# Prompt attention with closing banks freed by ScalarE, later combinations and evenly spread maximum units

## The reference

```python
def masked_softmax(s, mask):
    s = jnp.where(mask, s, NEG)
    m = jnp.max(s, axis=-1, keepdims=True)
    e = jnp.where(mask, jnp.exp(s - m), 0.0)
    return e / jnp.maximum(jnp.sum(e, axis=-1, keepdims=True), 1e-30)
...
    g = jax.nn.sigmoid(gates.astype(jnp.float32)).reshape(b, tq, NSA_GROUPS, HPG, 3)
    o = g[..., 0:1] * o_cmp + g[..., 1:2] * o_slc + g[..., 2:3] * o_win
```

## Time and profile before

| | us |
|---|---|
| median of 3 runs | 2638.7 (2637.68 to 2643.01) |
| profiled execution, device time | 2634.91 |
| profiled execution, span of instructions | 2633.1 |
| TensorE busy over the span | 2270.2 |
| stage of the prompt's attention | 446 to 803 |

### The profile page before, as it was taken

How to read it: one execution, slowest core, us unless ns; L and a number is a source line. 1 busy time by engine, 2 the same in 40 slices (tenths; PEclk the granted TensorE clock), 3 DMA queues, 4 the chain that set the end, 5 groups by cost and what they waited for, 6 DMA issues and landing times. The chain is left out here.

```text
span 2633.1 us, 32958 instructions
## 1 busy us (share of the span) xinstructions
PE 2270.2 (86%) x13162; PEld 1924.0 (73%) x13162; DVE 1049.5 (40%) x1988; ACT 556.9 (21%) x986; POOL 450.1 (17%) x174
## 2 busy tenths in 40 slices
PE   5598896888886878887779999797999999999997
PEld 3477684333335757887668888796998989898996
DVE  1754074454532222455511111415443444344345
ACT  2476163333331101111111110103111101101110
POOL 0211010133441001110011100212222212211120
PEclk9798897888896578988889999898999999999998
DMA  7111253000003222110123322212211111111101
GB/s 277 45 44 55 52 189 118 1 1 0 1 0 136 93 89 71 50 41 27 42 76 101 103 68 84 99 30 53 65 49 33 49 49 43 39 49 49 33 33 66
DMA packets 135814, 164.57 MB, mean 63 GB/s; under 512 B 11058, under 2 KB 108083, under 8 KB 131108
## 3 DMA queue, kind: packets, MB, share of 16 engines
q1 hardware_dynamic: 125366, 109.85, 13.8%
q0 software_dynamic: 7552, 48.16, 5.5%
q10 hardware_dynamic: 2768, 4.70, 0.5%
HBM read 149.10 MB, written 17.87 MB: 63 GB/s over the span
## 5 line engine op out<-in xcount | busy, mean ns | idle before, releaser
L242 PE MATMUL psall<-hT,ring_short 128*128 128x344 f32 x1536 | 506.3, 330 | 64.0 <-POOL ring_short L237 41.4
L244 PE MATMUL psall<-hT,ring_short 128*128 128x344 f32 x1536 | 499.2, 325 | 0.0
L243 PE MATMUL psall<-work_short,ring_short 128*128 128x344 f32 x1296 | 420.1, 324 | 14.4 <-issue 14.4
L237 POOL TENSOR_TENSOR ring_short<-ring,ring_short 128x2048 fp32r<-128x2048 f32 (+3 forms) x49 | 197.7, 4035 | 1028.9 <-DVE ring_short L232 1028.8
L242 PEld LDWEIGHTS psall<-hT,ring_short 128*128 128x128 f32 x1536 | 296.8, 193 | 66.7 <-issue 36.6
L244 PEld LDWEIGHTS psall<-hT,ring_short 128*128 128x128 f32 x1536 | 296.6, 193 | 14.9 <-issue 14.9
L243 PEld LDWEIGHTS psall<-work_short,ring_short 128*128 128x128 f32 x1296 | 248.4, 192 | 0.6
L2652 DVE SCALAR_TENSOR_TENSOR xT<-psall,mod,xT 128x344 f32<-128x344 f32 (+1 forms) x264 | 151.4, 573 | 129.6 <-PE psall L244 126.5
L242 PE MATMUL psall<-work_short,work_short 128*128 128x344 f32 x480 | 161.2, 336 | 0.0
L1087 POOL TENSOR_TENSOR ring<-ring 128x1024 f32<-128x1024 f32 x50 | 118.4, 2368 | 248.0 <-ACT ring L1230 193.6
L243 PE MATMUL psall<-xT_short,ring_short 128*128 128x344 f32 x480 | 158.7, 331 | 0.0
(11 more groups left out here) (381 smaller groups left out, 4045.9 us busy)
## 6 DMA issues: line engine op xcount, KB each, us to landing
ring<-in_ada_w SPq DMA_DIRECT2D x24, 1024.0 KB, 6.5
ring<-in_w_up SPq DMA_DIRECT2D x44, 512.0 KB, 5.0
ring<-in_w_in SPq DMA_DIRECT2D x20, 512.0 KB, 3.9
work<-in_w_down SPq DMA_DIRECT2D x10, 1024.0 KB, 4.9
x_spill<-xT SPq DMA_DIRECT2D x1, 4128.0 KB, 17.2
xT<-x_spill SPq DMA_DIRECT2D x1, 4128.0 KB, 14.5
work<-in_x_prompt ACTq DMA_DIRECT2D x1, 4096.0 KB
work<-in_w_in SPq DMA_DIRECT2D x8, 512.0 KB, 5.2
```

The lines of the kernel that those rows point to most:

```text
L237: return eng.tensor_tensor(lo, src, hi, ALU.subtract)
L242: pe.matmul(out, w[0], x[0], start=first, stop=False)
L243: pe.matmul(out, w[0], x[1], start=False, stop=False)
L244: return pe.matmul(out, w[1], x[0], start=False, stop=last)
```

## The change

- The close's bank is freed by ScalarE. `invert` first waits for the combination of the previous branch, copies the gates from PSUM to a new buffer `gate` in the work region (which grows by 512 columns to 26416), then takes the logarithm into `scaled` in the same region and signals `logged`; units three slots later wait for that. The exponential then runs in place in SBUF.
- `combine` multiplies `gate` and `scaled`, both now in SBUF.
- A combination is taken out before a max or turn whose slot is at least 4 past the close, instead of 2.
- The planner counts a max as 1, a turn as 0.25 and a split as 0; max and split are due 3 pairs ahead, a turn 1 pair ahead; at most 1.3 of cost go before each pair; and a turn may not stand directly behind a max of its own branch once its pairs are ahead.

```diff
-    due = [sum(1 for x in ahead if max(0, x[1].first - 2) <= i) for i in range(len(pairs))]
-    due = [max(n - 2 * j for j, n in enumerate(due[i:])) for i in range(len(pairs))]
+    cost = {"split": 0.0, "max": 1.0, "turn": 0.25}
+    late = {"split": 3, "max": 3, "turn": 1}
...
+    due = [max(n - 1.3 * j for j, n in enumerate(due[i:])) for i in range(len(pairs))]
...
-            if name == "turn" and w.index >= closed + 3:
+            if name == "turn" and (w.index >= closed + 3 or i and i < w.first and order[-1][:2] == ("max", w)):
                 break
...
                     if was == "close":
-                        pe.wait_ge(weighed, w.index + 1)
+                        pe.wait_ge(logged, w.index + 1)
...
-                pe.matmul(out[:, 1, :], pick[:, 1, :], shift[b.index % 3], start=True, stop=True)
+                pe.matmul(out[:, 1, :], pick[:, 1, :], shift[b.index % 3], start=True, stop=True).then_inc(gated, 1)
...
-                total = both[slot_of["close", b.index, 0] % 3][:, 0, :]
+                ps = both[slot_of["close", b.index, 0] % 3]
+                wait(act, combined, b.index)
+                act.wait_ge(gated, b.index + 1)
+                act.activation(gate, ps[:, 1, :], ACT.Copy)
                 act.wait_ge(summed, b.index + 1)
-                ch.link(act, act.activation(total, total, ACT.Ln, bias=tiny))
-                wait(act, combined, b.index)
-                act.activation(scaled, total, ACT.Exp, scale=-1.0).then_inc(rooted, 1)
+                act.activation(scaled, ps[:, 0, :], ACT.Ln, bias=tiny).then_inc(logged, 1)
+                act.wait_ge(logged, b.index + 1)
+                act.activation(scaled, scaled, ACT.Exp, scale=-1.0).then_inc(rooted, 1)
...
                 v.wait_ge(rooted, b.index + 1)
-                v.tensor_tensor(scaled, both[n][:, 1, :], scaled, ALU.mult).then_inc(weighed, 1)
+                ch.link(v, v.tensor_tensor(scaled, gate, scaled, ALU.mult))
                 v.wait_ge(pv, b.last + 1)
-                v.wait_ge(weighed, b.index + 1)
...
-                    while waiting and name in ("max", "turn") and slot_of["close", waiting[0].index, 0] + 2 <= n:
+                    while waiting and name in ("max", "turn") and slot_of["close", waiting[0].index, 0] + 4 <= n:
```

More of the change, by code:

```diff
@@ L158, in allocate @@
     s.ring, s.ring_short = region("ring", 8192)
-    s.work, s.work_short = region("work", 25904)
+    s.work, s.work_short = region("work", 26416)
     s.ident = sb("ident", [P, P], F32)
@@ L998, in attention_order @@
     pairs = [(b, i) for b in branches for i in range(b.n)]
-    due = [sum(1 for x in ahead if max(0, x[1].first - 2) <= i) for i in range(len(pairs))]
-    due = [max(n - 2 * j for j, n in enumerate(due[i:])) for i in range(len(pairs))]
+    cost = {"split": 0.0, "max": 1.0, "turn": 0.25}
+    late = {"split": 3, "max": 3, "turn": 1}
+    spent = [sum(cost[x[0]] for x in ahead[:n + 1]) for n in range(len(ahead))]
+    due = [sum(cost[x[0]] for x in ahead if max(0, x[1].first - late[x[0]]) <= i) for i in range(len(pairs))]
+    due = [max(n - 1.3 * j for j, n in enumerate(due[i:])) for i in range(len(pairs))]
     order, closed, done = [], 0, 0
     for i, (b, k) in enumerate(pairs):
-        while done < due[i]:
+        while done < len(ahead) and (spent[done] <= due[i] or ahead[done][1].first - late[ahead[done][0]] <= i):
             name, w, _ = ahead[done]
```

11 lines of the change are left out of this document (5 added, 6 removed).

## The result

| | before | after |
|---|---|---|
| median of the runs, us | 2639.5 (4 runs, 2637.7 to 2643.0) | 2596.7 (4 runs, 2590.4 to 2600.9) |
| profiled execution, span | 2633.1 | 2592.7 |
| stage, first maximum matmul to last close | 352.3 | 312.2 |

The stage became 40.1 us shorter and the span 40.4: what the stage gained came through to the end, and nothing else moved.

What follows compares the result with a forecast made beforehand. TensorE's idle time and clock in the stage 446 to 803 us bound it. Waits 42 - 32 = 10 us plus clock 7 gave -17: 2634.9 to 2618, plus 3.8 for the median, said as 2621.5; range 2600 to 2640.

Steps and rivals of the forecast that it cites:

- the walk of b17/b18: Step-by-step timing of one double close: first product ends 4.6, combined 6.1, waits 5.8 us against about 3.2 before.
- rival A: SBUF port not taken or adds missed, so VectorE's product isn't blocked: 34 us faster, 2604.5 us; chance 0.20.
- Rival B: ScalarE's serial chain at double closes, from the second gate copy, becomes the bound: 9.5 us slower, 2648; chance 0.15.
- C: Rival: waits only change place, from turns to spreads and cuts, and the clock falls as often: -3 us, 2636; chance 0.20.
- Clock: TensorE's low-clock time from 550 us on falls from 51 to 36 us: 7 us gained, bounds 0 and 20.
- new waits: Waits the change adds at double closes, singles and early units of the stage: 32 us, bounds 27 to 37.
- double close: Two branches closing together, at six places: 24.5 us of new waits in all, 4.1 each.
- singles: Single closes (b10, b13, b16, b19): the next score waits for the spread behind the combination, 1.1 us each, 4.4 in all.
- Early units: At b1, b2 and the cut of b6, copies wait behind deferred combinations: 3 us.
- Removed: TensorE waits that go: ten turn waits 22 us, bank waits 15.3, values and a query split 5; 42 us.
- price of the blocked product: VectorE's product of two SBUF operands waits for GpSimd's add: 1.0 us per double close, between 0 and 1.7.
- Evenly spread maxima remove no work: In the planner's order of maximum units: spreading them evenly was given no gain in the sum.

Runs made afterwards that it cites:

- e14: The changed kernel run again, nothing altered, as a control: 0.9841 of the kernel before, median 2601.4 us.
- e13: The kernel before with 8 filling bf16 matmuls ahead of each of ten late turn waits: 0.9877 of before, stage 339.5 us instead of 352.3.
- e9: The changed kernel with the planner of before (new close and combinations 4 slots after it kept): 1.0009 of the kernel before.
- e5: The changed kernel with turns due 3 pairs ahead and no rule against a turn directly behind its branch's maximum: 0.9946 of the kernel before.
- e7: The changed kernel with combinations taken out 2 slots after their close instead of 4: 0.9946 of the kernel before.
- e6: The changed kernel with up to 2 of cost ahead of each pair instead of 1.3: 0.9851 of the kernel before.
- e10: The changed kernel with the next block's query cut placed ahead of the last branch's turn: 0.9832 of the kernel before.
- e12: The changed kernel with own buffers for the compressed branch, the earlier query cut, and combinations 6 slots after the close: 0.9847 of the kernel before.

## Why the prediction was wrong, step by step

**Right.** TensorE's idle time and clock in one stage bound the change, and the stage's gain passed to the end: 40.1 of 40.4 us. All turn waits but those of b0 to b2 and b20 went, with 9.4 us left where about 12 were forecast; the bank waits by VectorE went. The product is blocked by adds: mean 1182 ns against "about 1.2 us", and the walk of b17/b18 came out as tabled above. So rival A's mechanism is refuted, though its 2604.5 us lies nearer to the result than my own number. Rival B's price was wrong, since the next pair's exponential ended almost none of TensorE's waits and a double close loses 3.5 us in the mean, not over 5.8. But its place was right: ScalarE's chain behind the second copy ends 14.7 of the 32.6 us of idle time that are left. C's exchange of waits did not happen.

**Wrong: the term "Clock", 7 us where the runs show about 20.** I took five low stretches of 7 us to remain late in the stage and sized the gain at 7 us, with 20 as a far bound. Over the whole stage the low time fell from 90.2 to 48.7 us, which is 21 us of work, and the mean of all executions gives about 20. One step that failed is that I counted from 550 us only: ahead of it the low time fell from 90.2 - 47.6 = 42.6 to 48.7 - 17.0 = 31.7 us (31 in e14), 5 to 6 us of work for which the sum had nothing. The other is what remains late. There the low time fell from 47.6 (I had 51) to 17.0 instead of 36, in four stretches of 3.4, 3.4, 3.4 and 6.8 us (the longest is the one at 684 us above). How far that step was off can't be told from one trace: e14, with the same waits, has five late stretches of 6.8, 3.4, 10.2, 6.8 and 3.4 us, 30.6 in all, one at each of the five late double closes, as I had it. By it the late clock gave 8.5 us, by the first trace 15. e13 shows that this clock is a price of its own.

**Wrong: the term "new waits", 32 us.** At the double closes, in the order of the prediction, the trace gives 4.9, 2.8, 2.7, 3.3, 1.8 and 5.3 = 20.8 us against 24.5, mostly because the query cut and the turn of b18 did not wait. The singles were sized at 4.4 and lost 1.3 us, only at b19: elsewhere the blocked product had ended before anyone needed VectorE. Early units: 3.8 against 3. That is 26 us instead of 32, so by my own sum 42 - 26 = 16 us of waits were gained, not 10. The measured fall of idle time is 21 us. The other 5 are waits of the kernel before that "Removed" had left out: of its 53.7 us only 6.1 (turns of b0 to b2) and 0.6 (the last close) stayed, so 47 us went where I had 42. Left out were 2.4 us of maximum matmuls without a visible releaser and 1.4 us of scores behind reductions (L1271); the rest is rounding and pieces under 0.5 us.

The price of the blocked product was bounded at 1.7 us, "a whole add". The longest one took 2.90 us, 2.2 more than alone; the mean of all 24 is 0.5 more.

**Wrong: "Evenly spread maxima remove no work".** The sum gave the planner's maxima nothing. e9 and e5 put what they and their earlier due times are worth, with turns left early, at 17 us.

**Wrong in its account: the deferral to 4 slots.** It stands in the prediction only as a cost, the combination of b18 ahead of maximum 4. At the single closes it is what lets the turn go without a wait: without it 29 us are lost (e7). The sum gave it no term, since I assumed the turn waits to be gone by the order alone. The forecast of 22 us "removed" therefore rests on two parts of the change, and it is right only because both are there.

**What stays open.** Whether it is the place of TensorE's code in its blocks that takes a stall out of the feed-forward network isn't tested; a kernel with the same number of instructions more but without filling in the waits would tell. How much low time a stage has in the mean can't be read from one trace of each kernel. Whether e6's spread and e10 to e12 are worth a few us can't be told from these runs.

## What to carry to other kernels

When one engine waits in several short pieces and its clock falls behind each, price the clock over the whole stage, and from more than one execution: here it was as large as the waits, and two traces of one kernel differed by 13 us of low time. Ask of every deferred operation what it would stand ahead of in its engine's queue under the new order as well as under the old one; the same constant was worth nothing in one order and 29 us in the other. And where a wait can't be removed, cheap matmuls into a free bank inside it may return what the clock loses behind it, 1.3 us for each wait of 2.2 us here. Then compare the other stages too: in the two kernels with filling matmuls a later stage of the same code was 12 to 16 us shorter, for another reason than the clock.

## What the runs showed of the hardware

The small operations suffer beside GpSimd too. In e7 the cast L232 of 128 x 8 values took 1.48 us and L1293 (a tensor and a constant) 2.20 us, each ending with an add of GpSimd (681.30 + 2.42 and 683.97 + 2.34); beside none they take 0.16 and 0.17. The Trainium skill, "SBUF — State Buffer", section Who interferes with whom, says of casts and of operations with one tensor and a scalar that they can enter a mode that takes the port pair shared with GpSimd. The trace agrees; the numbers are those just given.

A product of two SBUF operands that starts with an add waits for all of it: L1304 took 2.90 us at 709.45, and ended 0.56 us after the add (711.79).

TensorE's clock can be held with work that no one needs: 8 filling matmuls in each of ten waits cut the low time of the stage from 90.2 to 59.2 us. When it falls is not the same in every execution: with waits equal to 0.8 us in all, the changed kernel's stage had 48.7 and 61.7 us at 1.2 GHz.

In the feed-forward network TensorE lost 6 us at each of four places, in two stalls, each ending 1.3 to 1.8 us after a transfer of 16384 bytes of kind "instruction".
